# A hybrid decoder step on one core: tables loaded in parts, GLA scores taken with the queries stationary, and ScalarE issuing its loads before it splits weights

## The reference

```
mod = silu(c) @ w_ada + b_ada                    # six vectors of 2048: shift, scale, gate, twice
h   = rmsnorm(x) * (1 + scale1) + shift1
qa, ka, va, qb, kb, vb, r, glr = split(h @ w_in)
oa  = dilated windowed attention(qa, ka, va)     # 16 heads of 64, T5 bias, three dilations
a   = log_sigmoid(glr @ w_gate2 + b_gate2) / 16  # forget gate of GLA
att = (qb * exp(b)) (kb * exp(-b))^T, causal     # b: running sum of a; 4 heads, dk 128, dv 256
ob  = att @ vb + (qb * exp(b)) @ state;  state = decay * state + kd^T @ vb
x   = x + gate1 * (concat(rmsnorm(oa), rmsnorm(ob) * silu(r)) @ w_out)
x   = x + gate2 * conv_ffn(rmsnorm(x) * (1 + scale2) + shift2)
```

## Time and profile before

| what | value |
|---|---|
| time, median of 3 runs (lowest, highest) | 1621.52 us (1619.14, 1622.28) |
| profiled execution: its time, its span | 1621.12 us, 1619.6 us |
| PE busy | 1582.2 us (98%) |
| PEld, DVE, ACT busy | 88%, 55%, 41% |
| mean DMA rate | 229 GB/s |
| granted TensorE clock, mean | 0.994 |

### The profile page before, as it was taken

One profiled execution on the slowest core, in us unless ns is written; L12 is line 12 of the kernel. 1 busy time (PEld: TensorE's weight loads), 2 busy tenths in 40 slices (PEclk: granted clock), 3 DMA queues, 4 the chain that ended last, 5 costly groups with the idle time before them and its releaser, 6 DMA issues.

```text
span 1619.6 us, 29366 instructions
## 1 busy us (share of the span) xinstructions
PE 1582.2 (98%) x12352; PEld 1430.2 (88%) x12352; DVE 890.9 (55%) x1504; ACT 664.2 (41%) x925; POOL 76.9 (5%) x135
## 2 busy tenths in 40 slices
PE   8899999999999998999999999999999999999997
PEld 4677888888877765997999999999999999999997
DVE  3555555555665654657445455454555556656563
ACT  3332333343445434435334333343433445545452
POOL 2010000000111000000000000000000000000000
PEclk8999999999999999999999999999999999999999
DMA  9998877778877999866644444555545455555450
GB/s 339 375 384 298 307 258 260 270 278 282 288 255 278 335 397 368 310 231 235 229 163 158 158 161 156 182 163 175 161 158 168 148 170 179 160 177 179 158 183 27
DMA packets 240881, 370.81 MB, mean 229 GB/s; under 512 B 7809, under 2 KB 192483, under 8 KB 232553
## 3 DMA queue, kind: packets, MB, share of 16 engines
q1 hardware_dynamic: 216032, 279.88, 51.1%
q10 hardware_dynamic: 17538, 71.45, 11.8%
q0 software_dynamic: 7184, 17.64, 3.3%
HBM read 359.06 MB, written 9.88 MB: 228 GB/s over the span
## 4 chain that ended last, share of the span: by engine, by line
PE 83%; DMA 5%; issue 5%; DVE 4%; ACT 2%; SPq 1%; POOL 0%; ACTq 0%; POOLq 0%; DVEq 0%
PE ps L949 23%; PE ps L950 22%; PE ps L951 22%; PE ps L900 3%; PE ps L1197 2%; DMA ring<-in_w_in 1%; DMA ring<-in_w_ada 1%; DMA vals<-in_w_ada 1%; SPq L548 1%; DMA proj<-in_w_ada 1%; DVE wlo L2041 1%; PE ps L1212 1%; PE ps L1243 1%; PE ps L893 1%; DMA ring<-in_w_out 1%
## 5 line engine op out<-in xcount | busy, mean ns | idle before, releaser
L949 PE MATMUL ps<-hhi,whi 128*128 128x288 f32 x3120 | 929.7, 298 | 1.7 <-DVE hlo L2033 0.7
L950 PE MATMUL ps<-hlo,whi 128*128 128x288 f32 x3120 | 917.8, 294 | 0.0
L951 PE MATMUL ps<-hhi,wlo 128*128 128x288 f32 x3120 | 917.6, 294 | 0.0
L949 PEld LDWEIGHTS ps<-hhi,whi 128*128 128x128 f32 x3120 | 586.0, 188 | 40.1 <-issue 35.3
L950 PEld LDWEIGHTS ps<-hlo,whi 128*128 128x128 f32 x3120 | 586.2, 188 | 0.8
L951 PEld LDWEIGHTS ps<-hhi,wlo 128*128 128x128 f32 x3120 | 586.0, 188 | 0.0
L1897 DVE TENSOR_TENSOR wlo<-ring,whi 128x1024 fp32r<-128x1024 f32 x178 | 212.2, 1221 | 84.7 <-ACT whi L1479 84.3
L1479 ACT ACTIVATE whi<-ring 128x1024 fp32r<-128x1024 f32 x178 | 184.5, 1056 | 156.3 <-PE ps L951 156.3
L2041 DVE TENSOR_TENSOR wlo<-ring,whi 128x1024 fp32r<-128x1024 f32 x96 | 117.2, 1223 | 124.2 <-ACT whi L1488 124.0
L1488 ACT ACTIVATE whi<-ring 128x1024 fp32r<-128x1024 f32 x96 | 100.8, 1054 | 157.5 <-PE ps L951 125.4
L2541 DVE TENSOR_TENSOR wlo<-ring,whi 128x1024 fp32r<-128x1024 f32 (+1 forms) x94 | 105.7, 1131 | 56.0 <-ACT whi L1817 56.0
(11 more groups left out here) (318 smaller groups left out, 1115.7 us busy)
## 6 DMA issues: line engine op xcount, KB each, us to landing
ring<-in_w_up SPq DMA_DIRECT2D x88, 1024.0 KB, 5.1
ring<-in_w_ada ACTq DMA_DIRECT2D x58, 1024.0 KB, 7.2
ring<-in_w_in SPq DMA_DIRECT2D x48, 1024.0 KB, 8.8
ring<-in_w_down SPq DMA_DIRECT2D x32, 1408.0 KB, 6.6
ring<-in_cache_k_win SPq DMA_DIRECT2D x16, 1024.0 KB, 9.3
ring<-in_w_out SPq DMA_DIRECT2D x16, 1024.0 KB, 7.0
proj<-in_w_ada SPq DMA_DIRECT2D x14, 1024.0 KB, 9.4
ring<-in_w_ada SPq DMA_DIRECT2D x10, 1024.0 KB, 13.6
```

Source lines behind the costliest of these rows:

```text
L949: mm(out, w_hi, x_hi, start=start, stop=False)
L950: mm(out, w_hi, x_lo, start=False, stop=False)
L951: return mm(out, w_lo, x_hi, start=False, stop=stop)
```

## The change

1. *Tables.* The constant table is loaded in two parts. The first, 393 columns for the opening, is loaded first by SP; the second, 424 columns (masks of the GLA heads), by POOL later. POOL's wait ahead of this load and of the gate weights and the first head's states is now for the last turn of the opening (`turn_b` 3) and not for the one before it. The attention's table of multiplicities for old keys (640 columns of 128 rows) is replaced by two tables of 4 rows, which PE multiplies and adds to the bias products.
2. *ACT's order.* `late_rows`, `lead_load` and `late_load` stand ahead of `in_hi(j + 3)`.
3. *GLA.* `four_copies` is gone: the sample rows are turned once (L1076, L1087 of the changed kernel) and ACT and DVE copy them to the four partition groups. The scores are made with 32 query columns stationary and up to 256 key columns moving, each product in one of the four column groups; ACT copies the result out and PE turns it back (three turns).
4. *Waits.* The sum of r = 8 waits for the new states of b = 4 and 5 only; the next head's z waits for all.
5. *Small.* The gate's product, its copy and the fill of ones are one j later; four of the six idle products ahead of the up-projection are gone.

```diff
-        keep = CONST_LAYOUT["sum_groups"][0] + NC9
+        front, keep = CONST_LAYOUT["causal"][0], CONST_LAYOUT["own_batch"][0] + NB
...
-            sp.dma_start(con[:, :], a["tables"][:, 0:keep]).then_inc(con_in, 16)
+            sp.dma_start(con[:, 0:front], a["tables"][:, 0:front]).then_inc(con_in, 16)
...
-            pool.dma_start(temp[0:NBUCK, 0:c1 - c0], a["tables"][0:NBUCK, c0:c1]).then_inc(temp_in, 16)
+            pool.dma_start(temp[0:NBUCK, 0:ct - c0], a["tables"][0:NBUCK, c0:ct]).then_inc(temp_in, 16)
+            pool.dma_start(temp[0:TS, ct - c0:c1 - c0], a["tables"][0:TS, ct:c1]).then_inc(temp_in, 16)
...
-            pool.wait_ge(*AT.upto("turn_b", 2))
+            pool.wait_ge(*AT.upto("turn_b", 3))
             pool.wait_ge(fill_c, 1)
+            pool.dma_start(con[:, front:keep], a["tables"][:, front:keep]).then_inc(masks_in, 16)
...
-                mm(ps[:, 1, :], rel_rows, tview("hot_s", P)[:, 0:512], start=True, stop=True)
-                mm(ps[:, 2, 0:160], rel_rows, tview("hot_s", P)[:, 512:672], start=True,
+                mm(ps[:, 1, :], rel_rows, tview("hot_s", P)[:, 0:512], start=True, stop=False)
+                mm(ps[:, 1, :], tview("pick_t", TS), tview("mult_t", TS)[:, 0:512], start=False, stop=True)
+                mm(ps[:, 2, P:P + NS], rel_rows, tview("hot_s", P)[:, CK:CK + NS], start=True, stop=True)
+                mm(ps[:, 2, 0:P], rel_rows, tview("hot_s", P)[:, 512:CK], start=True, stop=False)
+                mm(ps[:, 2, 0:P], tview("pick_t", TS), tview("mult_t", TS)[:, 512:CK], start=False,
...
-                q = qp[:, 32 * c:32 * c + 32]
-                n = min(P, 32 * (c + 1))
-                last = mm(ps[0:n, 7, 32 * c:32 * c + 32], ki[c % 4][:, 0:n], q, start=True, stop=True)
-                if c >= 4:
-                    n = 32 * (c - 3)
-                    last = mm(ps[0:n, 7, P + 32 * c:P + 32 * c + 32], ki[c % 4][:, P:P + n], q, start=True,
-                              stop=True)
-                last.then_inc(*RT.step(f"att{c}"))
+                at, n, rows = P * (c // 4), 32 * (c + 1), slice(32 * (c % 4), 32 * (c % 4) + 32)
+                mm(ps[rows, 7, at:at + n], qp[:, 32 * c:32 * c + 32], ki[c % 4][:, 0:n], start=True,
+                   stop=True).then_inc(*RT.step(f"att{c}"))
+            def att_turns(h):
+                pe.wait_ge(*RA.upto("att_rows", h))
+                for n in range(3):
+                    last = turn(ps[:, 7, P * n:P * n + P], att_rows[:, P * n:P * n + P], ident)
+                last.then_inc(*RT.step("att_turned"))
...
-                        last = four_copies(ps[:, 6, P * e:P * e + P], proj[:, 32 + 2 * h + e, SEQ:TOK])
+                        last = turn(ps[0:NS, 6, P * e:P * e + P], proj[:, 32 + 2 * h + e, SEQ:TOK], ident)
...
-                    four_copies(ps[:, 4, SEQ:SEQ + P], kd[:, SEQ:TOK]).then_inc(*RT.step("kdrows"))
+                    turn(ps[0:NS, 4, SEQ:SEQ + P], kd[:, SEQ:TOK], ident).then_inc(*RT.step("kdrows"))
...
                     last.then_inc(*RT.step("os_rows"))
+                    att_turns(h)
...
-                    pe.wait_ge(*RV.upto("state1", h))
+                    pe.wait_ge(*RV.upto("state_half", h))
...
-                if j == 24:
+                if j == 25:
                     gate_rank()
...
-                    idle_products(2, 6)
+                    idle_products(2, 2)
...
-                    f(v_parts, ps[:, 6, 0:256], ACT.Copy)
+                    for g in range(4):
+                        f(v_parts[32 * g:32 * g + 32], ps[0:NS, 6, 0:256], ACT.Copy)
...
+                    act.wait_ge(*RT.upto("att7", h))
+                    f(att_rows, ps[:, 7, 0:384], ACT.Copy).then_inc(*RA.step("att_rows"))
...
-                if j + 3 < CH_OUT:
-                    in_hi(j + 3)
+                if j - 1 in LATE_AT[KD - 1::KD]:
+                    late_rows(LATE_AT.index(j - 1) // KD)
...
+                if j + 3 < CH_OUT:
+                    in_hi(j + 3)
...
-                    v.tensor_copy(kdr[:, 2, :], ps[:, 4, 256:384]).then_inc(*RV.step("kdr"))
+                    for g in range(4):
+                        last = v.tensor_copy(kdr[32 * g:32 * g + 32, 2, :], ps[0:NS, 4, 256:384])
+                    last.then_inc(*RV.step("kdr"))
...
-                    dve.wait_ge(*RT.upto("att7", h))
+                    dve.wait_ge(masks_in, 16)
+                    dve.wait_ge(*RT.upto("att_turned", h))
```

More of the change, by code:

```diff
@@ L91, in constants @@
     add("ones", np.ones((P, P), np.float32))
+    add("sum_groups", (np.arange(P)[:, None] % 32 == np.arange(NC9)[None]).astype(np.float32))
     s, c = np.arange(P)[:, None], np.arange(SEQ)[None]
@@ L106, in constants @@
     t = np.arange(TS)
+    add("pick_t", (t[:, None] == r[None] % TS).astype(np.float32))
+    add("mult_t", multiplicity(PAST + t[:, None] - pos[None]))
     add("hot_s", np.concatenate(
         [np.concatenate([one_hot(PAST + k - pos), one_hot(k - a % TS)], 1) for k in t], 0))
-    old = multiplicity(PAST + t[:, None] - pos[None])[r % TS]
     new = []
@@ L114, in constants @@
         new.append(np.where(b[:, None] == a[None] // TS, m, NEG))
-    add("mult_s", np.concatenate([old] + new, 1).astype(np.float32))
+    add("mult_s", np.concatenate(new, 1).astype(np.float32))
     return np.concatenate(parts, 1)
@@ L253, in build @@
         ki = [projf[:, t:t + 256] for t in (1698, 1954, 6304, 6560)]
+        att_rows = projf[:, 1698:2082]
         rb = projf[:, 2210:2219]
@@ L304, in build @@
         x_in = [sem(f"x_half_in{n}") for n in range(2)]
-        con_in, c_in, vec_in, rel_in, temp_in, wglr_in, wg2_in, vrow_in = (
-            sem(n) for n in ("con_in", "c_in", "vec_in", "rel_in", "temp_in", "wglr_in", "wg2_in",
+        con_in, masks_in, c_in, vec_in, rel_in, temp_in, wglr_in, wg2_in, vrow_in = (
+            sem(n) for n in ("con_in", "masks_in", "c_in", "vec_in", "rel_in", "temp_in", "wglr_in", "wg2_in",
                              "vrow_in"))
@@ L363, in build @@
         RT = st("gla_tensor", "z", "vrows", "att_s", *(f"att{i}" for i in range(4)), "kdrows",
-                *(f"att{i}" for i in range(4, 8)), "state", "os_rows", "o", "states0", "states1", "sum")
+                *(f"att{i}" for i in range(4, 8)), "state", "os_rows", "att_turned", "o", "states0", "states1", "sum")
         RV = st("gla_vector", "z", "la", "cum", "rb", "dq", "dd", "zero_att", "qp", "qe", "ke", "kd",
                 *(f"ki{i}" for i in range(4)), "kdr", "v_lo", *(f"ki{i}" for i in range(4, 8)), "att", "att_s", "kd_hi", "kd_lo", "kdm",
-                "state0", "state1")
+                "state0", "state_half", "state1")
         RN = st("gla_output", "ms", "o0", "o1")
@@ L370, in build @@
         RA = st("gla_scalar", "abs", "exp", "ln", "eq", "eqs", "eks", "ekd", "ekds", "dec", "vrows",
-                *(f"ki{i}" for i in range(8)), "stp", "os_rows", "sq", "lnr", "rs")
+                *(f"ki{i}" for i in range(8)), "att_rows", "stp", "os_rows", "sq", "lnr", "rs")
         RS = st("gla_gates", "r0", "r1")
@@ L857, in biases @@
             def biases():
-                pe.wait_ge(temp_in, 32)
+                pe.wait_ge(temp_in, 48)
                 pe.wait_ge(rel_in, 64)
@@ L1048, in new_states @@
                     last = mm(states(b), kdm[:, P * b:P * b + P], v_parts, start=True, stop=True)
-                return last
-            def four_copies(out, rows):
-                for g in range(4):
-                    last = mm(out[32 * g:32 * g + 32], rows, ident, start=True, stop=True)
                 return last
@@ L1060, in head @@
                     pe.wait_ge(wg2_in, 64)
+                    pe.wait_ge(*RV.upto("state1", h - 1))
                     mm(ps[:, 7, 0:TOK], wg2[:, P * h:P * h + P], glrT, start=True, stop=True).then_inc(*RT.step("z"))
@@ L1639, in _ @@
                         late_load(r)
-                if j == 25:
+                if j + 3 < CH_OUT:
+                    in_hi(j + 3)
+                if j == 26:
                     act.wait_ge(*GT.upto("done"))
@@ L1647, in _ @@
                     norm_hi(1 + ADA_AT[7::8].index(j - 2))
-                if j - 1 in LATE_AT[KD - 1::KD]:
-                    late_rows(LATE_AT.index(j - 1) // KD)
                 for h in range(H_B):
@@ L2156, in head @@
                         rows = slice(32 * g, 32 * g + 32)
-                        last = v.tensor_tensor(v_parts[rows], ps[rows, 6, 0:256], v_parts[rows].bitcast(F32), ALU.subtract)
+                        last = v.tensor_tensor(v_parts[rows], ps[0:NS, 6, 0:256], v_parts[rows].bitcast(F32), ALU.subtract)
                     last.then_inc(*RV.step("v_lo"))
@@ L2179, in head @@
                         last = new_state(b)
+                        if b == 5:
+                            last.then_inc(*RV.step("state_half"))
                     last.then_inc(*RV.step(f"state{r - 7}"))
@@ L2262, in _ @@
                     in_lo(j + 3)
-                if j == 27:
+                if j == 28:
```

9 lines of the change are left out of this document (4 added, 5 removed).

## The result

| | us, median | lowest to highest | runs | ratio to before (95% interval) |
|---|---|---|---|---|
| before | 1620.73 | 1619.14 to 1623.72 | 8 | |
| changed | 1624.12 | 1622.17 to 1627.89 | 8 | 1.0021 (1.0012 to 1.0030) |

The changed kernel is slower by 3.4 us, just over 0.2%. I had forecast 1620.0. The profiled execution took 1622.17 us with a span of 1620.6, the fastest of its runs, so the traces differ by less (1.0 us) than the medians.

A forecast was written before the change was run, and what follows sets the result against it. PE's own work was taken as four fifths of the chain, DMA and waits for ACT and DVE the rest. 1621.12 - 3.1 (opening) - 2.2 (heads) + 4.2 (pairs) = 1620.0 us; range 1615.5 to 1624.8.

The forecast's parts named there:

- ACT's order in pairs: Pairs after j = 74, 86 and 92: `whi` held behind loads or `late_rows` makes PE wait longer, +4.2 us.
- a falling clock: Sign of a wrong forecast: the clock falls from 1.0 where PE idles at the up-projection; no size given.
- Opening: Start to about 150 us: smaller tables, earlier loads and POOL's later wait shorten PE's slab waits, -3.1 us.
- rival 1: Opening: all 5.5 us of slab waits are given back instead of 3.1, total 1617.6 us; chance 0.25.
- Heads: GLA heads 0 to 3: single turns, faster score products and fewer state waits, less ACT's delay, -2.2 us.
- Idle products: Ahead of the up-projection: four fewer free 2 us of PE, which then waits for DVE instead, 0 us.
- the slower one: Held `whi` also costs one us each at j = 71, 77, 80, 83 and 89, total 1625.0 us; chance 0.14.
- the third: Heads: score products do not overlap or turns miss the fast mode; heads give 0, total 1622.2 us; chance 0.14.
- The low end of the range: 1615.5 us, given as the faster rival with the DMA hole filled as well.
- the hole's 1.2 us: DMA engines at 58 to 60 us run at 155 GB/s; filling this is worth 1.2 us, 0.3 taken.

The follow-up runs named there:

- two_joints_back: The changed kernel with the late loads behind `whi` again at j = 74 and j = 86 alone; 1617.26 us, ratio 0.9978.
- waits_filled: The changed kernel with idle products put into PE's waits behind j = 74 and j = 86; 1621.61 us, ratio 1.0001.
- opening_alone: late_order_back with the GLA part of the kernel before; 1619.32 us, ratio 0.9995.
- late_order_back: The changed kernel with late_rows and the late w_ada loads behind the next chunk's splitting again, opening loads left ahead; 1616.30 us, ratio 0.9977.
- bias_table_back: The changed kernel with the whole multiplicity table loaded and added by DVE again, as before; 1624.86 us, ratio 1.0029.
- after_again: The changed kernel, unaltered, timed and profiled once more; 1624.48 us, ratio 1.0024.
- keys_first: late_order_back with DVE scaling ki4 to ki7 ahead of kd's row copies, and PE making old states' products ahead of the state's; 1611.13 us.

## Why the prediction was wrong

The forecast was -1.1 us, measured was +3.4. By its own terms:

- **ACT's order in pairs, +4.2: the step that failed.** It priced the held `whi` at the waits alone, and these came nearly as forecast: 2.25 and 1.85 us in the first trace of the changed kernel, 2.6 and 1.9 in the second, against 1.86 and 1.8, and 0.48 at j = 92 against 0.5. The places were right too; two_joints_back gains 7.2 us from the first two. What was missing is what PE's standing still does behind them: the clock falls in part of the executions, 1.5 to 1.6 us a time, some 2.5 to 3 us of the median by waits_filled. I had named a falling clock as a way to be wrong, at another stage, and had given it no price.
- **Opening, -3.1.** Half right by its mechanisms. All 5.5 us of slab waits went, not 3.1, so rival 1 was right about the waits. But chunk 0 starts 2.3 us later, not 0.1 to 0.3 earlier: the bias products cost PE 1.9 us more, not 1.3, and a second stretch at the lower clock follows them at 36.4 us; and a wait for `hlo` of 1.5 us comes at 89 us. The trace has -2.1 at 150 us; opening_alone measures -1.25, and its interval holds 0.
- **Heads, -2.2.** The trace has -1.9 (from 2.1 ahead at 150 us to 4.0 at 420). The estimate held in the sum; that DVE's keys set r = 5 was right. What it did not see is how much stood there to be won. The three turns without the four-fold copies are as fast as it said (L1086 and L1087 take 0.55 us together at 243.22, their tail included).
- **Idle products, 0.** Right: the two traces keep their distance past 767 us.

Put together, the pairs cost 4.6 us of waits and 2.5 to 3 of falls, the opening gives 1.25 to 2.1 and the heads 1.9: +3.1 to +4.5, with +3.4 measured.

The mean granted clock of each run gives the time at the lower level (one less the clock, times two, times the span): 26 us on average over 89 runs of the kernel before, 33 over the 16 of the changed one, 28 in waits_filled, 27 in two_joints_back. At the 1.5 to 1.6 us lost per 3.4 us low, the 7 us more are some 3.3 us. This doesn't explain the result by itself: late_order_back has 31 us and is 4.5 us faster than before, with its second fall in the opening and the one in head 1. The clocks are given to 0.001, which is 1.5 us of loss in a single run, so only the averages say anything. That the falls at the pairs cause loss is shown by waits_filled. That the opening's does is not shown, and bias_table_back speaks against it.

Of the rivals, the slower one gave about the right time (1625.0) for a wrong reason. The score products do overlap (0.3 us for four, once the keys are there), and the turns' fast form holds, so the third falls. The low end of the range was not worked out right: 1617.6 less the hole's 1.2 us is 1616.4, not 1615.5; nothing hangs on it.

## What to carry to other kernels

A wait of TensorE costs more than its length where the granted clock falls behind it (here 1.5 to 1.6 us more for each fall); price a new wait of 1 to 3 us with that, and where it can't be avoided, fill it with products nobody needs. Before putting loads ahead of work on an in-order engine, list the few chunks where the next engine already waits: here two of them carried nearly all of the loss, and sparing them alone made the change pay. When a product is made faster, look at once at what feeds it; the order on the feeding engine was worth more (5 us or more, with the falls of the clock that it spared) than the faster product (3 us).

## What the hardware showed that I had not expected

- The granted clock falls after waits as short as 1.8 and 0.9 us close together, though not each time: the same joint shows it in after_again (2.29 us for L1132) and not in the first profile of the changed kernel (1.24).
- In head 1 the clock fell in four of five profiles behind a wait of 2.5 to 3.1 us, and in none of five behind one of 1.4 to 1.7 us.
- The low stretches in these traces are 3.4, 6.8, 10.2 or 13.7 us long, but for the last, which the program's end cuts off.
- Four score products (eight records, 32 weight columns each, 160 to 256 moving columns) into four column groups take 0.64 us with their tail, 0.3 to the next start (L1045 at 201.47, keys_first), when nothing spaces them.
